# Two-block transformer on one core: residual sums released bank by bank, the router norm per token tile, and half of the second expert's gate weights loaded ahead

## The reference, cut to what matters

```python
h = rmsnorm_2(x, norm1_g[l]) * (1.0 + sc1) + sh1
...
x = x + g1 * (merged @ w_out[l])
h2 = rmsnorm_2(x, norm2_g[l]) * (1.0 + sc2) + sh2
x = x + g2 * ec_moe(h2, w_router[l], w_gate[l], w_up[l], w_down[l])
```

## Time and profile before

| | us |
|---|---|
| median of 3 runs | 2524.04 |
| lowest, highest | 2520.86, 2524.99 |
| time of the profiled execution | 2518.5 |
| span of its profile | 2516.5 |
| PE busy, DVE busy, ACT busy, POOL busy | 2020.4, 912.3, 632.2, 32.0 |
| DMA moved | 641.86 MB, mean 255 GB/s |

### The profile page before, as it was taken

One profiled execution on the slowest core, in us unless ns is written; L12 is line 12 of the kernel. 1 busy time (PEld: TensorE's weight loads), 2 busy tenths in 40 slices (PEclk: granted clock), 3 DMA queues, 4 the chain that ended last, 5 costly groups with the idle time before them and its releaser, 6 DMA issues.

```text
span 2516.5 us, 35012 instructions
## 1 busy us (share of the span) xinstructions
PE 2020.4 (80%) x14440; PEld 1361.1 (54%) x14440; DVE 912.3 (36%) x1641; ACT 632.2 (25%) x1041; POOL 32.0 (1%) x50
## 2 busy tenths in 40 slices
PE   7877789998998997999876666665999886776665
PEld 6756557877755885888642222222878652222221
...
GB/s 312 103 1 35 2 113 151 262 239 198 361 201 167 219 258 204 160 144 101 167 228 426 427 427 426 426 426 405 152 146 118 172 186 427 427 426 427 427 425 282
DMA packets 150309, 641.86 MB, mean 255 GB/s; under 512 B 9310, under 2 KB 30840, under 8 KB 117046
## 3 DMA queue, kind: packets, MB, share of 16 engines
...
## 4 chain that ended last, share of the span: by engine, by line
PE 55%; DMA 32%; DVE 6%; ACT 3%; issue 2%; DVEq 1%; POOL 1%; SPq 0%; ACTq 0%; POOLq 0%
DMA ring<-in_w_down 31%; PE psum L1249 5%; PE psum L873 5%; PE psum L875 5%; PE psum L874 5%; PE psum L1364 4%; PE psum L971 3%; PE psum L645 2%; PE psum L1239 2%; PE psum L852 2%; PE psum L1127 1%; PE psum L1129 1%; PE psum L1128 1%; PE psum L988 1%; PE psum L676 1%
## 5 line engine op out<-in xcount | busy, mean ns | idle before, releaser
L1344 PE MATMUL psum<-ring,arena 128*32 128x256 f32 x4096 | 296.7, 441 | 185.7 <-DMA ring<-in_w_up 146.4
L1344 PEld LDWEIGHTS psum<-ring,arena 128*32 128x32 f32 x4096 | 143.6, 123 | 341.2 <-issue 154.8
L1364 PE MATMUL psum<-ring,arena 128*32 128x512 f32 x1024 | 166.8, 784 | 94.6 <-DMA ring<-in_w_down 85.4
L873 PE MATMUL psum<-arena_r 128*128 128x512 f32 x512 | 208.7, 408 | 13.9 <-DVE arena_r L1710 7.1
L2071 DVE TENSOR_TENSOR arena<-psum,arena 128x256 f32<-128x256 f32 x32 | 13.6, 425 | 558.2 <-PE psum L1344 558.2
L875 PE MATMUL psum<-ring_r,arena_r 128*128 128x512 f32 x512 | 206.1, 402 | 0.0
L1444 DVE TENSOR_TENSOR ring_r<-ring,arena_r 128x2048 fp32r<-128x2048 f32 x64 | 143.7, 2288 | 86.2 <-ACT arena_r L2129 86.1
L2495 ACT ACT_TABLE_LOAD x32 | 41.1, 1283 | 515.2 <-PE psum L1344 515.2
L2078 DVE COPY arena<-psum 128x512 f32<-128x512 f32 x64 | 44.3, 692 | 273.4 <-PE psum L1364 272.3
L2129 ACT CAST arena_r<-ring 128x2048 fp32r<-128x2048 f32 x64 | 119.5, 1902 | 71.1 <-PE psum L875 71.1
L1364 PEld LDWEIGHTS psum<-ring,arena 128*32 128x32 f32 x1024 | 32.7, 126 | 192.1 <-DMA ring<-in_w_down 101.8
...
## 6 DMA issues: line engine op xcount, KB each, us to landing
...
```

The source lines that it names most:

```text
L873: mm(o, xh, wh, start=start, stop=False, skip_group_check=True)
L1344: ins = mm(PS[32 * j:32 * j + 32, 4 + m, 0:T], XGE[:, 4 * u + kk, :], W(v + 2 * m + u, D)[:, kk, j * T:(j + 1) * T], start=u == 0 and kk = ...
L1364: ins = mm(PS[32 * j:32 * j + 32, (7, 4)[half], :], HTE[:, k % 2, 32 * (k // 2):32 * (k // 2) + 32], W(v + 4 + u, D)[:, j, half * 512:(hal ...
```

## The change

1. PE raises `half_mm` twice per projection, at the end of bank 1 and of bank 2. `residual` and `gated_residual` wait for bank 2 alone before they touch it, and for the whole projection only before bank 3.
2. DVE squares tile 1 in two halves (`square_part`), each right after the sum of its bank; `mean_square` then adds the two partial sums. This holds after the four `residual` and after w_out, not after the experts.
3. The norm in front of the router is split by tile: PE turns tile 0 into banks 4 and 5 and tile 1 into 6 and 7, ACT moves all of tile 0 and half of tile 1, DVE the other half, and the router of tile 0 runs once tile 0 is in HT. SCL and BIA are computed before the sum.
4. SP loads gate 0 and gate 1 of expert 1 into free SBUF (NEXT0, NEXT1) right behind expert 0's weights; the last part goes over HT and waits for the router. ACT copies them into the ring slots after its work for expert 0. The ring itself then goes on with up 0 of expert 1. Expert 0 is taken out of ACT's loop, experts 0 and 1 out of SP's.

```diff
@@ -362,6 +362,8 @@
         HE = c(T)
         HTE = c(2, P)
         YS = c(2, 512)
+        NEXT0 = ar[:, 16384:16384 + SLOT]
+        NEXT1 = [HT[:].rearrange("p k t -> p (k t)"), WPOOL.rearrange("p g c -> p (g c)"), OT.rearrange("p a t -> p (a t)")]
...
+
+                def expert(e, first):
...
-                            load(U_SEC + V_MOE + 2 * m + u, pmajor(two(A[name]))[:, 4 * u:4 * u + 4, :], tu + e)
+                            if 2 * m + u >= first:
+                                load(U_SEC + V_MOE + 2 * m + u, pmajor(two(A[name]))[:, 4 * u:4 * u + 4, :], tu + e)
...
+                expert(0, 0)
+                second = pmajor(one(A["w_gate_2"])[1])
+                sp.dma_start(NEXT0.rearrange("p (k n) -> p k n", n=D), second[:, 0:4, :]).then_inc(sem("next0_in"), 16)
+                for part, ks in ((1, slice(6, 7)), (2, slice(7, 8))):
+                    sp.dma_start(NEXT1[part].rearrange("p (k n) -> p k n", n=D), second[:, ks, :]).then_inc(sem("next1_in"), 16)
+                sp.wait_ge(sem("router_mm"), L + 1)
+                sp.dma_start(NEXT1[0].rearrange("p (k n) -> p k n", n=D), second[:, 4:6, :]).then_inc(sem("next1_in"), 16)
+                expert(1, 2)
+                with sp.Fori(2, NE) as e:
+                    expert(e, 0)
...
-            def norm_split(k, t):
+            def norm_split(k, t, pm=False):
...
                     ins = nc.tensor.transpose(PS[:, 4 + 2 * t + dc // 4, (dc % 4) * P:(dc % 4 + 1) * P],
-                                              XN[:, t, dc * P:(dc + 1) * P], ident)
+                                              by_rows(t)[:, dc] if pm else XN[:, t, dc * P:(dc + 1) * P], ident)
...
-                    if last and (kk, b) == (cnt - 1, 1):
+                    if last and kk == cnt - 1 and b in (1, 2):
                         ins.then_inc(sem("half_mm"), 1)
...
+                def router(t):
+
+                    for k in range(KC):
+                        ins = mm(PS[:, 4, t * NE:(t + 1) * NE], HT[:, k, t * P:(t + 1) * P], WR[:, k, :], start=k == 0, stop=k == KC - 1)
+                    return ins
...
-                norm(L * 2 + 5, True)
-                normed(L * 2 + 7)
                 for t in range(TT):
-                    for k in range(KC):
-                        ins = mm(PS[:, 4, t * NE:(t + 1) * NE], HT[:, k, t * P:(t + 1) * P], WR[:, k, :], start=k == 0, stop=k == KC - 1)
-                ins.then_inc(sem("router_mm"), 1)
+                    norm_split(L * 2 + 5, t, True)
+                    if t == 1:
+                        pe.wait_ge(sem("ht0_ready"), L + 1)
+                        router(0)
+                pe.wait_ge(sem("ht_ready"), L * 16 + 48 + 16)
+                router(1).then_inc(sem("router_mm"), 1)
...
+            def square_part(h):
+
+                xs = X[:, 1, h * 512:(h + 1) * 512]
+                v.tensor_tensor_reduce(out=XN[:, 1, h * 512:(h + 1) * 512], in0=xs, in1=xs, scale=1.0, scalar=0.0,
+                                       op0=ALU.mult, op1=ALU.add, accum_out=ssq_parts[:, h:h + 1])
+
+            def mean_square(r, meanwhile=None, parts=True):
+
+                if parts:
+                    settle()
+                    v.tensor_tensor(ssq[:, 1:2], ssq_parts[:, 0:1], ssq_parts[:, 1:2], ALU.add)
...
             def residual(n, complete):
 
-                dve.wait_ge(sem("half_mm"), n)
+                dve.wait_ge(sem("half_mm"), 2 * n - 1)
                 for b in range(4):
                     t, h = b // 2, b % 2
                     if b == 2:
-                        ins.then_inc(sem("x_half"), 1)
+                        dve.wait_ge(sem("half_mm"), 2 * n)
+                    elif b == 3:
                         complete()
                     xs = X[:, t, h * 512:(h + 1) * 512]
                     ins = v.tensor_tensor(xs, bank(b), xs, ALU.add)
-                ins.then_inc(sem("x_ready"), 1)
+                    if b == 1:
+                        ins.then_inc(sem("x_half"), 1)
+                    elif b == 3:
+                        ins.then_inc(sem("x_ready"), 1)
+                    if b >= 2:
+                        settle()
+                        square_part(h)
...
-            def gated_residual(n, tile1_ready):
+            def gated_residual(n, tile1_first, tile1_ready, parts):
...
                     ins = v.tensor_tensor(xs, xs, TMP, ALU.add)
                     if b == 1:
                         ins.then_inc(sem("x_half"), 1)
+                    elif b == 3:
+                        ins.then_inc(sem("x_ready"), 1)
+                    settle()
+                    if b >= 2 and parts:
+                        square_part(h)
+                    if b == 1:
+                        tile1_first()
+                    elif b == 2:
                         tile1_ready()
-                    elif b < 3:
-                        settle()
-                ins.then_inc(sem("x_ready"), 1)
                 settle()
...
-                dve.wait_ge(sem("half_mm"), L + 5)
-                gated_residual(L * 2 + 1, lambda: (settle(), spent(dve, u2 + V_OUT + 1, tu)))
-
-
                 v.scalar_tensor_tensor(SCL, mc(4), 1.0, PMC[:, bass.ds(L * 8 + PM_AT["norm2_g_2"], 8)], ALU.add, ALU.mult)
                 v.tensor_copy(BIA, mc(3))
-                settle()
-                norm(L * 2 + 6, L * 2 + 7, lambda dc: SCL[:, dc:dc + 1], lambda dc: BIA[:, dc:dc + 1])
+                dve.wait_ge(sem("half_mm"), L * 2 + 9)
+                gated_residual(L * 2 + 1, lambda: dve.wait_ge(sem("half_mm"), L * 2 + 10), lambda: spent(dve, u2 + V_OUT + 1, tu), True)
+
+                mean_square(L * 2 + 6)
+                v.tensor_scalar(XN[:, 1, :], X[:, 1, :], rstd[:, 1:2], None, ALU.mult).then_inc(sem("xn1"), 1)
+                dve.wait_ge(sem("ht_psum"), L * 3 + 9)
+                for dc in range(4, KC):
+                    v.tensor_scalar(HT[:, dc, P:T], PS[:, 7, (dc % 4) * P:(dc % 4 + 1) * P], SCL[:, dc:dc + 1], BIA[:, dc:dc + 1],
+                                    ALU.mult, ALU.add).then_inc(sem("ht_ready"), 1)
...
-                norm(L * 2 + 6, L * 2 + 7, L * 2 + 6, lambda dc: SCL[:, dc:dc + 1], lambda dc: BIA[:, dc:dc + 1])
+                mean_square(L * 2 + 6, L * 2 + 6)
+                act.wait_ge(sem("rstd_ready"), (L * 2 + 6) * 2 + 1)
+                a.activation(XN[:, 0, :], X[:, 0, :], ACT.Copy, scale=rstd[:, 0:1]).then_inc(sem("xn0"), 1)
+                for t in range(TT):
+                    act.wait_ge(sem("ht_psum"), L * 3 + 8 + t)
+                    for dc in range(KC - 4 * t):
+                        ins = a.activation(HT[:, dc, t * P:(t + 1) * P], PS[:, 4 + 2 * t + dc // 4, (dc % 4) * P:(dc % 4 + 1) * P],
+                                           ACT.Identity, scale=SCL[:, dc:dc + 1], bias=BIA[:, dc:dc + 1])
+                        if t == 1:
+                            ins.then_inc(sem("ht_ready"), 1)
+                    if t == 0:
+                        ins.then_inc(sem("ht0_ready"), 1)
...
+
+                expert(0)
+                gate0, gate1 = u2 + V_MOE, u2 + V_MOE + 1
+                act.wait_ge(sem("next0_in"), L * 16 + 16)
+                a.copy(ring[gate0 % RING][:, 0:SLOT], NEXT0).then_inc(w_full[gate0 % RING], 16)
+                act.wait_ge(sem("next1_in"), L * 48 + 48)
+                at = 0
+                for part in NEXT1:
+                    ins = a.copy(ring[gate1 % RING][:, at:at + part.shape[1]], part)
+                    at += part.shape[1]
+                ins.then_inc(w_full[gate1 % RING], 16)
+                with act.Fori(1, NE) as e:
+                    expert(e)
```

31 lines of the change are left out of this document (15 added, 16 removed).

## The result

| | before | changed |
|---|---|---|
| median, first comparison | 2522.96 (4 runs) | 2488.59 (4 runs) |
| lowest, highest | 2520.86, 2524.99 | 2485.63, 2494.55 |
| ratio of the times, 95% interval | | 0.9869, 0.9853 to 0.9884 |
| all runs of this study: median, mean | 2520.7, 2520.9 (72 runs) | 2489.3, 2490.6 (15 runs) |
| profiled execution, its span | 2518.5, 2516.5 | 2489.25, 2487.2 |

The changed kernel is faster: by 34.4 us in the first comparison, by 30 to 31 us (1.2%) over all runs. The direction was right, the size was not. One further run of the kernel before, in a slow state (3046.76 us at a granted clock of 0.63), is not in these numbers.

A forecast was written before the change was run, and what follows sets the result against it. DMA was taken to bound the two expert plateaus, a chain through PE, DVE, ACT and POOL the time between. 2 x (6.6 + 4.4 - 0.1) + 2.6 = 24.4 us off 2524.04 gave 2499.6, range 2490 to 2509.

The forecast's parts named there:

- Term 1: Expert plateaus of both layers: two weight units of expert 1 loaded ahead save 6.6 us per layer, between 4.5 and 6.6.
- Term 2: From w_out to the router: norm split by tile, router ends 4.4 us earlier per layer (3.0 to 5.0).
- the clock comes back late: Before the zeroing: clock returns late, zeroing to gather run at half rate, at most 20 us per layer, 2539.7; chance 0.03.
- the clock stays up at the router: At the router's norm and router: PE's clock does not fall, up to 4.2 us more per layer, 2491.2; chance 0.08.
- the slack of 1.4 us: Under the router: ACT's copy and table load and DVE's subtraction end 1.4 us early; any overrun would reduce the gain.
- Term 3: First block's norms: bank 2's sum and half a square of tile 1 move earlier, 2.6 us, from 1.5 to 3.5.
- rival at 2512.8: Expert plateaus: weight stream breaks by 6.6 us or more, preload worth nothing, 11.2 us gain left, 2512.8; chance 0.08.

The follow-up runs named there:

- b1: Changed kernel with three products of zeros on PE between the turns of tile 0 and tile 1 of the router's norm; 2489.5 us, 0.9881 of before.

## Why the forecast was wrong in size

**The sum against the means of all profiles.** One pair of profiles was not enough to size terms of 2 to 6 us, so here are the means over all 17, by the code that a stage has:

| stage | old code | new code | gain | forecast |
|---|---|---|---|---|
| plateau, each layer | 460.3 (10 values, 458.9 to 460.7) | 451.9 (20, 451.1 to 455.1) | 8.4 | 6.6 - 0.1 |
| head, each layer | 46.1 (12, 44.3 to 48.4) | 41.8 (14, 38.9 to 43.5) | 4.3 | 4.4 |
| norm behind MLP 0 to the one behind the window attention | 192.1 (5, 190.1 to 193.5) | 189.0 (10, 187.8 to 190.2) | 3.1 | 0.95 |
| that norm to the one behind MLP 1 | 208.6 (6, 207.4 to 209.2) | 207.3 (11, 206.7 to 208.0) | 1.3 | 0.7 |
| norm behind MLP 1 to the next | 9.11 (6) | 8.27 (11) | 0.84 | 0.95 |
| start to the norm behind the gated delta net | 376.9 (17, 372.8 to 383.9), same code | | 0 | 0 |

**Term 1 is the step that failed**: it was sized at 6.6 us per layer ("between 4.5 and 6.6"), and the plateaus became 8.4 us shorter. What it did count held: 4.91 us per unit, the issue at S + 5.4, the copies in time, nothing broken. DMA's stream at full rate ends 6.5 us earlier behind S: at 2491.25 (S + 446.2) before and 2464.75 (S + 439.7) after. Clock and share of DMA (second number from the end) in the pieces behind that, of before and of the changed kernel:

```profile
2491.25:2493.25 2.00, 0.00 (x0) 0.00 (x0) 0.00 (x0) 0.00 (x0) 0.00 (x0) 1.00 0.17 70
```

```profile
2464.75:2465.25 0.50, 0.00 (x0) 0.00 (x0) 0.00 (x0) 0.00 (x0) 0.00 (x0) 1.00 0.41 164
2465.25:2466.00 0.75, 0.07 (x4) 0.07 (x8) 0.00 (x0) 0.00 (x0) 0.00 (x0) 1.00 0.00 0
```

What the sum left out stands behind it, 1.8 us per layer in the mean (8.4 against 6.6). The last unit trickles in over 2 us at a 17% share before and over half a microsecond after: 1.3 us of the pick-up in this pair, 0.9 us more than the term in the mean of all. And the tail takes 10.3 us more often than 11.9: about 0.9 us in the mean, 1.56 where the two tails differ. I had read the 4.4 us between 90 units and the last pick-up as "start and landing", the same on both sides, and put the top of the bounds at my own value. In layer 1 of all 7 profiles with 90 or 89 units in the stream DMA's share lies at 0.04 to 0.08 from 2.0 to 1.0 us before the pick-up, about the share of one of the 16 engines (an estimate: 1/16 is 0.06); in the 10 with 88 units it is 0.79 or more there. In layer 0 other transfers run there and hide it. Why it is so was not tried and stays open.

**Term 2 came out** (4.4): the heads are 4.3 us shorter in the mean. The work was sized well: POOL's power of tile 1 comes 5.04 us behind that of tile 0 instead of 7.37, 2.3 us for the forecast's 2.4. That the mean fits so closely is in part luck, since two things that the term did not have cancel. In 9 of 14 heads tile 1 was still turned at full clock (1.16 to 1.25 us for 1.97), and the router's end came up to 5.7 us earlier instead of 4.7. And the long zeroing was drawn in 7 of 14 heads of the new code and in 4 of 12 of the old. The first pair shows 3.2 and 3.4 us, because its old heads have the short zeroing and its new ones the middle one; the old code has the middle one too, in 4 of 12 heads, so the new gap need not be its cause. The rival "the clock comes back late" thus came true in part, in the heads with the long zeroing, and the old code has them as well: 4 us against the shortest heads, far from the 12.2 per layer from which it decides (its time, added up, is 2539.6). The rival "the clock stays up at the router" came true for the turn of tile 1 alone: the router took 6.63 to 6.85 us in all 14 heads. b1 shows that its price was right, 3.72 against my 3.7, and that its 4.2 us would not have come, since DVE's subtraction then holds up the softmax: the slack of 1.4 us that term 2 names ran out, as it said.

**Term 3** (2.6) has the right size where its work can be seen: 0.84 and 0.85 for 0.95 each, and the powers in 0.55 us each, by which ACT's scaling of tile 0 starts 0.58 us behind the power and no longer 1.36 (768.67 behind 768.09, 774.41 behind 773.05): 0.78 for 0.7. The stages around the window attention gained more, 3.1 and 1.3, but their values overlap with the old ones or lie within what one code varies by. In the time nothing of the term can be told from zero.

**The base.** It was the median of three runs, 2524.04; 72 runs give 2520.7. 3.3 us of the 11 were in this number, and the miss in gain is rather 6 to 7 us (30.3 by the means, 31.4 by the medians, against 24.4) than 10. Of these, term 1 is 3.8. The rest, 2 to 3, lies within what identical code varies by. So does the last step out of the range: the three medians of the changed kernel are 2488.6, 2488.6 and 2493.0, and the range begins at 2490.

**The preload was not worthless** (rival at 2512.8): without it (a3) the time is 2508.2, with one unit (b3) 2505.2, with both 2489.3, and the plateaus are 460.6, 457.4 and 451.9 us.
